# The second feed-forward product by block products, with the modulation pairs placed elsewhere

## What is computed

```python
def layer(x, cond, p, ctx):
    mod = (jax.nn.silu(cond) @ p['w_mod'] + p['b_mod'])[:, None, :]
    shift1, scale1, gate1, shift2, scale2, gate2 = jnp.split(mod, 6, axis=-1)
    h = rms_norm(x, p['norm1_g']) * (1 + scale1) + shift1
    out, ctx_out = mixer(h, p, ctx)
    x = x + gate1 * out
    h2 = rms_norm(x, p['norm2_g']) * (1 + scale2) + shift2
    x = x + gate2 * (jnp.square(jax.nn.relu(h2 @ p['w_ff1'])) @ p['w_ff2'])
    return x, ctx_out
```

## Time and profile before

| what | value |
|---|---|
| median of 3 runs | 2070.89 us |
| lowest and highest | 2069.68 and 2074.9 us |
| the profiled execution, its own time | 2063.75 us |
| its span | 2062.0 us |
| TensorE busy, matmuls | 1980.4 us (96%), 13976 |
| VectorE busy | 1217.4 us (59%) |
| ScalarE busy | 946.0 us (46%) |
| GpSimd busy | 284.7 us (14%) |
| granted clock of TensorE, mean | 0.992 |

### The profile page before, as it was taken

One profiled execution on the slowest core, in us unless ns is written; L12 is line 12 of the kernel. 1 busy time (PEld: TensorE's weight loads), 2 busy tenths in 40 slices (PEclk: granted clock), 3 DMA queues, 4 the chain that ended last, 5 costly groups with the idle time before them and its releaser, 6 DMA issues.

```text
span 2062.0 us, 34108 instructions
## 1 busy us (share of the span) xinstructions
PE 1980.4 (96%) x13976; PEld 1810.8 (88%) x13976; DVE 1217.4 (59%) x2095; ACT 946.0 (46%) x1746; POOL 284.7 (14%) x229
## 2 busy tenths in 40 slices
...
GB/s 367 74 51 11 1 27 52 114 166 128 188 81 112 144 91 150 68 149 88 158 109 74 36 6 1 47 58 120 163 162 124 51 89 65 94 62 103 62 94 60
DMA packets 53035, 195.92 MB, mean 95 GB/s; under 512 B 6032, under 2 KB 8144, under 8 KB 52112
## 3 DMA queue, kind: packets, MB, share of 16 engines
...
...
## 4 chain that ended last, share of the span: by engine, by line
PE 82%; DVE 11%; ACT 3%; issue 2%; DMA 2%; SPq 0%; ACTq 0%; DVEq 0%
PE ps L742 36%; PE ps L894 23%; PE ps L809 2%; PE ps L914 2%; PE ps L1060 2%; PE ps L923 2%; DVE w_lo_parts L1687 2%; PE ps L760 2%; PE ps L1036 2%; PE ps L847 2%; PE ps L1090 2%; PE ps L1065 1%; ACT scratch L1508 1%; DVE scratch L2095 1%; DVE merged L1764 1%
## 5 line engine op out<-in xcount | busy, mean ns | idle before, releaser
L1687 DVE TENSOR_TENSOR w_lo_parts<-w_raw,w_hi_parts 128x512 fp32r<-128x512 f32 x548 | 403.9, 756 | 242.9 <-ACT w_hi_parts L1274 148.2
L1274 ACT CAST w_hi_parts<-w_raw 128x512 fp32r<-128x512 f32 x296 | 172.1, 619 | 457.5 <-PE ps L742 413.4
L742 PE MATMUL ps<-hid_hi_parts,w_hi_parts 128*128 128x320 f32 x1216 | 280.3, 312 | 2.3 <-DVE merged L2154 1.6
L742 PE MATMUL ps<-hid_lo_parts,w_hi_parts 128*128 128x320 f32 x1216 | 277.0, 309 | 0.0
L742 PE MATMUL ps<-hid_hi_parts,w_lo_parts 128*128 128x320 f32 x1216 | 276.9, 309 | 0.0
L1885 DVE SCALAR_TENSOR_TENSOR x<-ps,modulation,x 128x128 f32<-128x128 f32 (+2 forms) x216 | 81.7, 434 | 319.0 <-PE ps L742 319.0
L742 PEld LDWEIGHTS ps<-hid_hi_parts,w_hi_parts 128*128 128x128 f32 x1216 | 201.9, 188 | 25.3 <-issue 22.1
L1278 ACT CAST w_hi_parts<-w_raw 128x512 fp32r<-128x512 f32 x252 | 152.2, 621 | 137.5 <-PE ps L742 56.7
L742 PEld LDWEIGHTS ps<-hid_lo_parts,w_hi_parts 128*128 128x128 f32 x1216 | 203.3, 188 | 0.0
L742 PEld LDWEIGHTS ps<-hid_hi_parts,w_lo_parts 128*128 128x128 f32 x1216 | 203.3, 188 | 0.0
L894 PE MATMUL ps<-h_hi_parts,w_hi_parts 128*128 128x320 f32 x560 | 173.8, 310 | 0.0
...
## 6 DMA issues: line engine op xcount, KB each, us to landing
...
```

The lines of the kernel that those rows point to most:

```text
L742: ins = mm(out[:, h, :], weight(w, s, k), a[:, k, h * HALF:(h + 1) * HALF], start=(first and n == 0), stop=(last and n == 2))
L1274: copy(place(wh, r), raw_half(s, n)).then_inc(w_hi, 1)
L1687: return tt(dst, full, hi.bitcast(F32), ALU.subtract)
```

## The change

The second product of blocks 1 and 2 and the first four tiles of that of block 3 are multiplied two tiles at a time: hidden rows 0 to 3 by seven block products of 6 matmuls, rows 4 to 7 whole, 48 matmuls. A pair has six *pieces* of weights (piece 4 half as wide as the others) where two whole tiles had four halves. The two waits inside are for ScalarE's copies of P1, P5 and U2, as rows 4 to 7 are added into the same banks. Finished tiles are put together by VectorE in `gqk` and then added to `x`. The four differences of the hidden rows 0 to 3 are made by VectorE in step 2 of the pairs for rows 2 and 4 of the first product, cast by ScalarE and split by VectorE in the pairs for rows 4 and 6. GpSimd makes four sums of half the size for each pair. `hid_cols` leaves out the right half of hidden rows 0 and 1 from cast and subtraction in blocks 1 and 2, where no product reads it.

Layer 0's modulation pairs move: the eight in the second products of blocks 1 and 2 are gone from there; five more stand in the mixer (after q = 2 of m = 1, 2, 4, 5, 6), one more in the output product, two more in the second product of block 0.

The diff, cut to its core:

```diff
-        return int(q == 0 or q == 2 and m in (3, 7))
-    if OUT0 < i <= OUT0 + (4 if l == 0 else 2):
+        return int(q == 0 or q == 2 and (m in (3, 7) or l == 0 and m > 0))
+    if OUT0 < i <= OUT0 + (5 if l == 0 else 2):
         return 1
     if l == 0 and i - FF0 in (1, 2):
         return 1
-    if l == 0 and FF0 + KT < i < FF0 + 48:
-        return int((i - FF0) % 16 in (9, 10, 12, 13))
+    if l == 0 and FF0 + KT <= i < FF0 + KT + 6:
+        return 1
...
+def by_parts(s):
+
+    f, q = divmod(s % PER - FF0, 2 * KT)
+    return f >= 1 and KT <= q < (2 * KT if f < FF_BLOCKS - 1 else KT + 4)
...
+PIECES = 6
+STEPS = 10
+USED_UP = (2, 4, 5, 7, 8, 10)
...
+def part_pairs(f):
+
+    return range(0, (0, KT, KT, 4)[f], 2)
+
+
+def whole_second(f):
+    return range((0, KT, KT, 4)[f], KT if f < FF_BLOCKS - 1 else KT - 2)
...
+        def part_moving(f, n):
+
+            at_ = {0: (0, 0), 1: (2, 0), 5: (2, 1)}
+            if n in at_:
+                k, h = at_[n]
+                return uh[:, k:k + 2, half_cols(h)], ul[:, k:k + 2, half_cols(h)]
+            d = {2: 0, 3: 1, 4: 2, 6: 3}[n]
+            return hid_diff_hi(f, d), hid_diff_lo(d)
+
+        def hid_cols(f, q):
+
+            return half_cols(0) if f in (1, 2) and q < 2 else slice(0, TOK)
...
+        def piece_source(s, n):
+
+            return (raw_half(s, 0), s1_sb[0], raw_half(s, 1), raw_half(s, 0), raw_half(s + 1, 0)[:, 2:4, :],
+                    raw_half(s + 1, 1))[n]
...
+            def sums_used(s):
+
+                if s in AHEAD and leads(AHEAD[s]):
+                    pool.wait_ge(block_lo, BLOCK[AHEAD[s]] + 3)
+                elif s in AHEAD:
+                    pool.wait_ge(part_lo, PIECES * PART[AHEAD[s]] + 2)
+
+            def part_sums(s):
+
+                s1, s3 = s1_sb[0][:, 0:2, :], s1_sb[0][:, 2:4, :]
+                a11, a12 = raw_half(s, 0)[:, 0:2, :], raw_half(s, 0)[:, 2:4, :]
+                a21, a22 = raw_half(s + 1, 0)[:, 0:2, :], raw_half(s + 1, 0)[:, 2:4, :]
+                for t in (s, s + 1):
+                    r = PLACE["main", t]
+                    pool.wait_ge(raw_in[r % RAW], 16 * (r // RAW + 1))
+                sums_used(s)
+                nc.gpsimd.tensor_tensor(s1, a21, a22, ALU.add).then_inc(part_sum, 1)
+                nc.gpsimd.tensor_tensor(s3, a11, a21, ALU.subtract).then_inc(part_sum, 1)
+                pool.wait_ge(part_lo, PIECES * PART[s] + 1)
+                pool.wait_ge(part_sum, 4 * PART[s] + 2)
+                nc.gpsimd.tensor_tensor(a11, s1, a11, ALU.subtract).then_inc(part_sum, 1)
+                pool.wait_ge(part_sum, 4 * PART[s] + 3)
+                nc.gpsimd.tensor_tensor(a12, a12, a11, ALU.subtract).then_inc(part_sum, 1)
...
+            def pair_in_parts(f, q, o):
+
+                s = e.layer * PER + FF0 + 2 * KT * f + KT + q
+                r, no = RING[s], PART[s]
+                n = o + KT + q
+
+                def read(used):
+                    pe.wait_ge(pair_free[used % 2], e.at(pair_free[used % 2], used // 2 + 1))
+
+                def piece_ready(p):
+                    pe.wait_ge(part_lo, PIECES * no + p + 1)
+
+                def block(c, p, at_row):
+                    hi, lo = part_moving(f, c)
+                    for k in range(2):
+                        for j, (w, a) in enumerate(((wh, hi), (wh, lo), (wl, hi))):
+                            last = mm(ps[:, block_bank(s, c), 0:HALF], place(w, r + p)[:, at_row + k, :], a[:, k, :],
+                                      start=(c < 4 and k == 0 and j == 0), stop=(k == 1 and j == 2),
+                                      skip_group_check=True)
+                    last.then_inc(part_mm, 1)
+
+                def lower(bank, p, h, ks, start):
+                    for k in ks:
+                        if q == 0:
+                            pe.wait_ge(hid_ready, e.at(hid_ready, KT * f + k + 1))
+                        for j, (w, a) in enumerate(((wh, uh), (wh, ul), (wl, uh))):
+                            last = mm(ps[:, bank, 0:HALF], place(w, r + p)[:, k - 4, :], a[:, k, half_cols(h)],
+                                      start=(start and k == 4 and j == 0), stop=(k == ks[-1] and j == 2),
+                                      skip_group_check=True)
+                    return last
+
+                def diff_made(d):
+                    pe.wait_ge(hid_diff_ready, e.at(hid_diff_ready, 4 * (f - 1) + d))
+
+                b = [block_bank(s, c) for c in range(4)]
+                piece_ready(0)
+                read(n - 3)
+                pe.wait_ge(hid_ready, e.at(hid_ready, KT * f + 2))
+                block(0, 0, 0)
+                pe.wait_ge(hid_ready, e.at(hid_ready, KT * f + 4))
+                block(1, 0, 2)
+                piece_ready(1)
+                read(n - 2)
+                diff_made(1)
+                block(2, 1, 0)
+                if q == 0:
+                    read(n - 1)
+                else:
+                    pe.wait_ge(part_sums_read, 2 * no)
+                diff_made(2)
+                block(3, 1, 2)
+                piece_ready(2)
+                lower(b[1], 2, 0, range(4, 6), False)
+                pe.wait_ge(part_copied, 3 * no + 2)
+                lower(b[2], 2, 1, range(4, 6), False)
+                lower(b[1], 2, 0, range(6, KT), False)
+                lower(b[2], 2, 1, range(6, KT), False).then_inc(part_mm, 1)
+                piece_ready(3)
+                diff_made(3)
+                pe.wait_ge(part_copied, 3 * no + 1)
+                block(4, 3, 0)
+                block(5, 3, 2)
+                piece_ready(4)
+                diff_made(4)
+                pe.wait_ge(part_sums_read, 2 * no + 1)
+                block(6, 4, 0)
+                piece_ready(5)
+                lower(b[3], 5, 0, range(4, KT), False).then_inc(part_mm, 1)
+                pe.wait_ge(part_copied, 3 * no + 3)
+                lower(b[0], 5, 1, range(4, KT), True).then_inc(part_mm, 1)
+                modulation(s % PER)
+                modulation(s % PER + 1)
...
-                        pair_by_sevens(n, i + q, {0: n - 2, 2: n - 1} if first else {0: n - 4, 2: n - 2, 3: n - 1})
-                    for q in range(KT if f < FF_BLOCKS - 1 else KT - 2):
+                        pair_by_sevens(n, i + q, {0: n - 2, 2: n - 1} if first and f < 2 else {0: n - 3, 2: n - 2, 3: n - 1})
+                    for q in part_pairs(f):
+                        pair_in_parts(f, q, o)
+                    for q in whole_second(f):
...
-                act.wait_ge(hid_ready, e.at(hid_ready, KT * f + q - 1))
+                act.wait_ge(hid_ready, e.at(hid_ready, KT * f + (q if q in (2, 4) else q - 1)))
                 fn(hid[:, q % 2, :], gqk[:, q % 2, :], ACT.Square).then_inc(hid_sq, 1)
                 act.wait_ge(hid_sq, e.at(hid_sq, KT * f + q + 1))
-                copy(uh[:, q, :], hid[:, q % 2, :]).then_inc(hid_hi, 1)
+                cols = hid_cols(f, q)
+                copy(uh[:, q, cols], hid[:, q % 2, cols]).then_inc(hid_hi, 1)
+
+            def cast_hid_diff(f, n):
+                act.wait_ge(hid_diff, e.at(hid_diff, 4 * (f - 1) + n + 1))
+                copy(hid_diff_hi(f, n), hid_full(n)).then_inc(hid_cast, 1)
+
...
+            def pair_in_parts(f, q, o):
+
+                s = e.layer * PER + FF0 + 2 * KT * f + KT + q
+                r, no, n = RING[s], PART[s], o + KT + q
+                p1, p5, u2, _ = copies(s)
+                act.wait_ge(part_mm, STEPS * no + 1)
+                act.wait_ge(pair_free[n % 2], e.at(pair_free[n % 2], n // 2))
+                copy(p1, ps[:, block_bank(s, 0), 0:HALF]).then_inc(part_copied, 1)
+                cast_entry(r + 4)
+                act.wait_ge(part_mm, STEPS * no + 3)
+                copy(p5, ps[:, block_bank(s, 2), 0:HALF]).then_inc(part_copied, 1)
+                cast_entry(r + 5)
+                cast_entry(r + 6)
+                act.wait_ge(part_mm, STEPS * no + 6)
+                copy(u2, ps[:, block_bank(s, 0), 0:HALF]).then_inc(part_copied, 1)
+                for c in range(7, 10):
+                    cast_entry(r + c)
+                if f == FF_BLOCKS - 1:
+                    for t in (q, q + 1):
+                        act.wait_ge(pair_free[t % 2], e.at(pair_free[t % 2], (o + KT + t) // 2 + 1))
+                        square(t)
...
+                    if n == 0 and first and f >= 2:
+                        act.wait_ge(pair_free[o % 2], e.at(pair_free[o % 2], o // 2))
                     pair_step(e.layer * PER + FF0 + 2 * KT * f + q, n)
                     if n == 1 and not first:
                         hid_by_sevens(f, q - 1, o)
+                    if f > 0 and (q, n) in ((4, 4), (4, 5), (6, 4), (6, 5)):
+                        cast_hid_diff(f, {(4, 4): 0, (4, 5): 1, (6, 4): 2, (6, 5): 3}[q, n])
...
                     hid_by_sevens(f, KT - 1, o)
-                    for q in range(KT if f < FF_BLOCKS - 1 else KT - 2):
+                    for q in part_pairs(f):
```

(59 more changed lines are left out.)

117 lines of the change are left out of this document (86 added, 31 removed).

## The result

The changed kernel takes 2088.13 us (median of 4 runs, 2086.81 to 2089.79), the kernel before on the same chip 2070.28 us (2069.11 to 2074.9). The ratio is 1.0098, 95% interval 1.008 to 1.0116: **slower by 17.9 us**, against a forecast of 13.6. The profiled execution of after took 2086.81 us (span 2085.0).

A forecast was written before the change was run, and what follows sets the result against it. TensorE, busy 96% of the span, was taken to bound the kernel. -17.6 + 2.6 + 9.4 + 19.2 = +13.6 us on the median of 2070.89 gave 2084.5, say 2085 us; the range was 2066 to 2097.

The forecast's parts named there:

- Matmuls, -17.6: Second products in parts: six matmuls fewer a pair, 120 in 20 pairs, at 0.147 us each, saving 17.6 us.
- Modulation pairs, +2.6: Layer 0's mixer: five more steps with a modulation pair, each 0.5 us longer through load waits; 2.6 us more.
- the bound of 6: Upper bound, in us, on the cost of moving modulation pairs into layer 0's mixer; the lower was 0.
- Steady pairs, 0: Pairs in parts: VectorE's and ScalarE's added work is covered by TensorE's 13.2 us; 0, bounds 0 and 0.5 us a pair.
- Ahead of the seventh product, +9.4: Rows 4/5 of the first product: VectorE's subtractions delay a sum TensorE awaits; 1.4 us in blocks 1 and 2, 1.9 in block 3.
- At the hand-over, +19.2: Start of the second product in parts: TensorE waits for ScalarE's copy of P5; 3.2 us in each of six blocks.
- The walk: Hand-over estimate with VectorE and GpSimd taking turns and half-size sums of 0.7 us: a standstill of 3.8 us.
- the paragraph on the clock: It said the hand-over standstill comes in two or three parts, 3 to 4 us together, between busy stretches.
- gaps of 2 to 4 us: Expected sign: one or more such TensorE gaps in each second product's first 9 us, the last released by ScalarE's copy.
- What is late next is nothing: Behind the waiting copy of P5, a cast and the copy of U2, wanted 6 us later, catch up without further delay.
- The clock, 0: Hand-over: no fall of TensorE's clock was assumed, as TensorE is busier there than in the second norm of layer 0.
- The rival's price: The clock falls at the hand-over: 1.5 us in each of six blocks, 9 us in all, giving 2094; chance 0.12.

The follow-up runs named there:

- hidden_first: handover_later with bank reads leading to hidden rows 6 and 7 put first on VectorE, two difference casts behind row 7, copies P1/P5 before row 7's cast: ratio 0.9971, 2062.29 us.
- diffs_more: The changed kernel with a dose more: one 0.82 us subtraction made twice in the run of four before the seventh product's sum; ratio 1.0141.
- copies_first: The changed kernel with ScalarE's copies of P1 and P5 in the first pair in parts put ahead of hidden row 7; ratio 1.008.
- diffs_later: The changed kernel with the hidden-row differences made one step later, behind VectorE's sum for the seventh product; ratio 1.0083.
- handover_later: The changed kernel with copies_first's order, GpSimd's sums held back, piece 3's cast and subtraction behind row 7, differences behind the seventh product's sum; ratio 1.002.
- diffs_pool: The changed kernel with the three subtractions of hidden rows 2/3 made by GpSimd in place of VectorE; ratio 1.0143.

## Why the prediction was right, and where it was off

- **Matmuls, -17.6:** 120 fewer, and pairs in parts at 13.2 us without a wait, as forecast. `hidden_first` shows the saving itself: 2.3 of 3.5 us arrive in each of blocks 1 and 2, and none of the 1.8 in block 3, so 9 of the 17.6.
- **Modulation pairs, +2.6:** 3.0 in the profile. A step of the mixer with the new pair and no turn takes 21.73, 22.18 and 22.53 us, where 22.1 was forecast; one with a turn 22.7 to 22.9. (The rows show one of each, from first pair to first pair.)
```profile
439.89:462.07 22.18, 22.05 (x149) 1.00 0.50 182
462.07:484.94 22.87, 22.80 (x157) 1.00 0.48 174
```
What the forecast put at nothing comes behind these steps: the mixer's last tile and the output product take 3.0 us more for one pair of 1.1, with two waits for VectorE (0.8 us at 534.01, 0.7 at 544.81) that the kernel before does not have. The run of this part alone says 6.8, interval 4.1 to 9.5, so even 3.0 may be too small; the bound of 6 was the better guess. If so, it is in part luck that the account comes as near to the medians as it does.
- **Steady pairs, 0:** no wait in any.
- **Ahead of the seventh product, +9.4:** 1.4 and 1.9 us a block, as worked out, with the releaser named. The dose run shows the cause.
- **At the hand-over, +19.2:** the mis-sized term. A block loses 5.3 - 1.4 = 3.9 us there, in block 3 likewise 5.9 - 1.9 = 4.0: 23.6 us in place of 19.2. The walk with VectorE and GpSimd taking turns gave 3.8; I took 3.2, on the hope that their order would save one collision. It saved none. The walk was also too simple: it has one standstill, at the copy of P5 (the paragraph on the clock speaks of two or three parts, and not of what they wait for). There are three, and two of them are waits for banks that VectorE reads late. None of the three distances is longer than 1.84 us, where gaps of 2 to 4 us were named as the sign; only together do the three cost 3.3 to 3.6 us. The wait for the copy of P5 alone, taken away in `copies_first`, is worth 0.8 us in block 1 of layer 1 and in block 3, and between nothing and 1.3 in the others.
- **"What is late next is nothing"** held for the changed kernel: behind the copy of P5 no distance in block 1 of layer 0 is above 0.4 us. It says nothing of what is late once a wait is gone, and each run that took away one wait found the next: 1.4 us a block taken away, 0.4 won (`diffs_later`), 1.4 to 1.7 and 0.8 (`copies_first`), 1.4 and 0.2 (`handover_later`). My reading after `diffs_later`, that VectorE is full in this stretch whatever the order, fell with `hidden_first`, which has the same work on it and wins 4.0 us a block. It was the order, that of the hand-over, together with GpSimd's sums falling into it, in shares that no run separates.
- **The clock, 0:** no fall cost anything in the changed blocks of after, whose waits are 0.6 to 2.0 us; the single one, at 1802.0 in layer 1, leaves its block as long as the next (both 107.36): the wait for the copy of P5 is shorter there by about as much (0.57 us from start to start, where the next block has 1.84). The rival's price was right for the matmuls, 1.5 us a time, of which 0.9 is left in the block where it could be compared. Longer waits bring it more often: at 2.8 us the clock fell in five blocks of six in `diffs_pool` and behind one wait of two in `diffs_more`. It is no sharp edge: `copies_first`, with no wait above 1.6 us in block 1 of layer 0, has a fall at that hand-over (794.1) too, and `diffs_later` has one at each of two hand-overs.

The account's 18.4 us are 4.8 above the forecast of 13.6: 4.4 from the hand-over, 0.4 from the modulation pairs.
